# Gate and up weights loaded in runs of eight rows a partition: a decoder layer with a mixture of experts on one core

## What is computed

```python
t = x.reshape(bsz * s, d)                       # 512 x 1024, layer norm 1 done
g_logits = t @ router_group_w + router_group_b  # 4 groups: one is taken
e_logits = t @ router_expert_w + router_expert_b  # 32 experts: two of the group are taken
...
hg = jnp.einsum("td,edf->tef", t, exp_w_gate)   # gate and up weights: 32 x 1024 x 256 each
hu = jnp.einsum("td,edf->tef", t, exp_w_up)
hid = jax.nn.silu(hg) * hu * combine[:, :, None]
out = jnp.einsum("tef,efd->td", hid, exp_w_down)  # down weights: 32 x 256 x 1024
...
h = layer_norm(DEEPNORM_ALPHA * h + ffn, ln2_g, ln2_b)
```

## Time and profile before

| | |
|---|---|
| runs | 436.12, 437.76, 437.44 us |
| median | 437.44 us |
| profiled execution | 435.74 us, span of the trace 433.9 us |
| PE matmul busy | 409.5 us (94%) |
| PE weight loads busy | 276.5 us (64%) |
| VectorE, ScalarE, GpSimd busy | 187.3, 114.6, 83.5 us |
| mean granted PE clock | 0.983 of full speed |
| HBM read, written | 134.41 MB, 12.58 MB |

### The profile page before, as it was taken

How to read it: one execution, slowest core, us unless ns; L and a number is a source line. 1 busy time by engine, 2 the same in 40 slices (tenths; PEclk the granted TensorE clock), 3 DMA queues, 4 the chain that set the end, 5 groups by cost and what they waited for, 6 DMA issues and landing times.

```text
span 433.9 us, 6632 instructions
## 1 busy us (share of the span) xinstructions
PE 409.5 (94%) x2578; PEld 276.5 (64%) x2578; DVE 187.3 (43%) x368; ACT 114.6 (26%) x185; POOL 83.5 (19%) x113
## 2 busy tenths in 40 slices
PE   7999999999999999999999999999999878888793
PEld 6888877888888888865555555556555544453331
DVE  3569522699955388854222122212221212111077
ACT  4442387953132003211111111111111101001411
POOL 2220000000000001122332333233323311210124
PEclk9999999999999999999999999999999989898997
DMA  8865532033379999999999999999999999999584
GB/s 276 268 192 181 190 98 77 22 97 98 97 251 415 415 412 421 415 375 408 406 406 409 410 405 408 409 408 406 411 412 410 409 413 411 412 412 417 217 332 193
DMA packets 45569, 139.11 MB, mean 321 GB/s; under 512 B 5107, under 2 KB 17427, under 8 KB 41446
## 3 DMA queue, kind: packets, MB, share of 16 engines
q1 hardware_dynamic: 39376, 126.89, 75.3%
q0 software_dynamic: 6144, 11.84, 7.5%
q10 hardware_dynamic: 22, 0.02, 0.0%
HBM read 134.41 MB, written 12.58 MB: 339 GB/s over the span
## 4 chain that ended last, share of the span: by engine, by line
PE 80%; DMA 11%; DVE 5%; SPq 2%; issue 1%; ACT 0%; DVEq 0%; ACTq 0%
PE bank L1088 21%; PE bank L902 12%; PE bank L903 12%; PE bank L904 12%; PE bank L1117 10%; DMA wgu<-in_exp_w_up 5%; DMA wgu_first<-in_exp_w_up 5%; PE bank L1078 3%; PE bank L1108 2%; SPq L500 2%; PE bank L1179 2%; DVE stats L1572 1%; PE bank L885 1%; PE bank L1055 1%; PE bank L962 1%; DMA raw<-in_w_in 1%
## 5 line engine op out<-in xcount | busy, mean ns | idle before, releaser
L1088 PE MATMUL bank<-wgu,xTg 128*64 128x256 f32 x736 | 87.9, 394 | 7.5 <-DMA wgu<-in_exp_w_up 6.7
L1088 PEld LDWEIGHTS bank<-wgu,xTg 128*64 128x64 f32 x736 | 52.9, 141 | 35.2 <-DMA wgu<-in_exp_w_up 7.6
L902 PE MATMUL bank<-xT_hi,w_hi 128*128 128x512 f32 x160 | 63.0, 394 | 0.9 <-DVE xT_lo L1228 0.9
L903 PE MATMUL bank<-xT_lo,w_hi 128*128 128x512 f32 x160 | 62.4, 390 | 0.0
L904 PE MATMUL bank<-xT_hi,w_lo 128*128 128x512 f32 x160 | 62.4, 390 | 0.0
L1528 DVE TENSOR_TENSOR hid<-gated,bank 64x256 f32<-64x256 f32 x32 | 13.5, 423 | 112.1 <-ACT gated L834 112.0
L674 POOL DMA_INDIRECT y_pairs<-ys,y_rows x32 | 32.5, 1016 | 140.7 <-PE bank L1078 105.1
L834 ACT ACTIVATE gated<-bank 64x256 f32<-64x256 f32 x32 | 12.1, 377 | 136.8 <-PE bank L1088 136.8
L1117 PE MATMUL bank<-wdn,hidT 128*64 128x512 f32 x192 | 45.4, 593 | 0.0
L1205 DVE TENSOR_TENSOR w_lo<-raw,w_hi 128x2048 fp32r<-128x2048 f32 x12 | 27.5, 2288 | 26.6 <-ACT w_hi L748 26.6
L669 POOL DMA_INDIRECT xg<-h_rows,x_rows x31 | 31.4, 1014 | 24.7 <-issue 8.3
(11 more groups left out here) (255 smaller groups left out, 499.0 us busy)
## 6 DMA issues: line engine op xcount, KB each, us to landing
wgu<-in_exp_w_gate SPq DMA_DIRECT2D x24, 1024.0 KB, 19.9
wgu<-in_exp_w_up SPq DMA_DIRECT2D x24, 1024.0 KB, 21.8
wdn<-in_exp_w_down SPq DMA_DIRECT2D x24, 1024.0 KB, 21.5
raw<-in_w_in SPq DMA_DIRECT2D x9, 1024.0 KB, 5.3
raw<-in_w_out SPq DMA_DIRECT2D x4, 1024.0 KB, 5.0
wdn_extra<-in_exp_w_down SPq DMA_DIRECT2D x4, 1024.0 KB, 22.2
wgu_spare<-in_exp_w_gate SPq DMA_DIRECT2D x4, 1024.0 KB, 18.9
wgu_spare<-in_exp_w_up SPq DMA_DIRECT2D x4, 1024.0 KB, 21.2
```

The source lines that it names most:

```text
L902: pe.matmul(dst, a_hi, b_hi, start=start, stop=False)
L903: pe.matmul(dst, a_hi, b_lo, start=False, stop=False)
L1088: mm = pe.matmul(psum[2 + b][BLOCK * which:BLOCK * which + BLOCK, 0:F], xTg[b][:, j, h * BLOCK:(h + 1) * BLOCK], wgu[s][:, which, k, :], s ...
```

## The change

Gate and up weights are read as `(p k) f`: partition `p` gets rows 8p to 8p+7, one run of 8 KB. What multiplies them has to have the same order, so that step `k` of partition `p` is column 8p + k of the layer norm's result. The change gets it by writing that result in another order of columns: the left half of a row holds, for each `m` of 128, columns 8m to 8m+3, the right half columns 8m+4 to 8m+7. `h1_rows`, the gathers, `turn_x`, `take_first` and the products of the experts are as before and get the new order by that. It touches:

- `gu_of`, `gu_place`: the loads' form.
- the layer norm: L1363 writes to a new tile `scaled` (4 KB a partition more), and L1368 reads `scaled` and `ln_b` in the dealt order and writes `xres` contiguously.
- `turn_h1`: a transpose takes every fourth column, as in `turn_x`; the router's weights are loaded `(p k) n`.
- L1179: `h1` is read through `in_order`, which takes four floats from one half and four from the other by turns.

```diff
--- before.py
+++ after.py
@@ -165,6 +165,7 @@
         hidT = [sb(f"hidT{b}", [P, 2, BLOCK]) for b in range(2)]
         ys = [sb(f"ys{b}", [P, H]) for b in range(ROWS)]
         xg = [sb(f"xg{b}", [P, H]) for b in (1, 0)][::-1]
+        scaled = sb("scaled", [P, D])
         gelu_g = at("gelu_g", [P, CT, T], F32, shared)
         h1T = [at(f"h1T{b}", [P, KT, P], F32, shared + 4096 * b) for b in range(2)]
         shared_y = shared + 8192
@@ -407,6 +408,14 @@
         def static(i):
             return isinstance(i, int)
 
+        def dealt(rows, a):
+
+            return rows[:, :].rearrange("p (m a j) -> p a m j", a=2, j=4)[:, a, :, :]
+
+        def in_order(rows):
+
+            return rows.rearrange("p (a m j) -> p m a j", a=2, j=4)
+
         def halves_of(rows, n):
 
             return rows.rearrange("p (m j) -> p m j", j=4)[:, :, 2 * n:2 * n + 2]
@@ -414,14 +423,14 @@
 
         def gu_of(w, e):
             w = w[e:e + 1] if static(e) else w[bass.ds(e, 1)]
-            return w.rearrange("a (h p j) f -> p (a h) (j f)", h=2, p=P)
+            return w.rearrange("a (p k) f -> p (a k f)", p=P)
 
         def dn_of(e):
             w = exp_w_down[e:e + 1] if static(e) else exp_w_down[bass.ds(e, 1)]
             return w.rearrange("a (p j) d -> p (a j d)", p=P)
 
         def gu_place(s, which):
-            return wgu[s][:, which, :, :].rearrange("p (h j) f -> p h (j f)", h=2)
+            return wgu[s][:, which, :, :].rearrange("p k f -> p (k f)")
 
 
 
@@ -637,9 +646,9 @@
             pool.dma_start(ln_b[:, :], row(ln1_b).to_broadcast([P, D])).then_inc(ln1_in, 16)
             pool.wait_ge(gates_in, 32)
             pool.wait_ge(ln1_in, 32)
-            pool.dma_start(wr[:, :, 0:N_GROUPS], router_group_w.rearrange("(k p) n -> p k n", p=P)).then_inc(router_in, 16)
+            pool.dma_start(wr[:, :, 0:N_GROUPS], router_group_w.rearrange("(p k) n -> p k n", p=P)).then_inc(router_in, 16)
             pool.wait_ge(router_in, 16)
-            pool.dma_start(wr[:, :, N_GROUPS:NR], router_expert_w.rearrange("(k p) n -> p k n", p=P)).then_inc(router_in, 16)
+            pool.dma_start(wr[:, :, N_GROUPS:NR], router_expert_w.rearrange("(p k) n -> p k n", p=P)).then_inc(router_in, 16)
             pool.dma_start(rbias[:, 0:N_GROUPS], row(router_group_b).to_broadcast([P, N_GROUPS])).then_inc(router_in, 16)
             pool.dma_start(rbias[:, N_GROUPS:NR], row(router_expert_b).to_broadcast([P, N_EXP])).then_inc(router_in, 16)
 
@@ -995,7 +1004,8 @@
                 for n in halves:
                     pe.wait_ge(h1_ready, 2 * t + n + 1)
                     for k in range(4):
-                        mm = pe.transpose(psum[4 + 2 * (t % 2) + n][:, k * P:(k + 1) * P], xres[:, t, (4 * n + k) * P:(4 * n + k + 1) * P], ident[:, :])
+                        cols = xres[:, t, n * H:(n + 1) * H].rearrange("p (m j) -> p j m", j=4)[:, k, :]
+                        mm = pe.transpose(psum[4 + 2 * (t % 2) + n][:, k * P:(k + 1) * P], cols, ident[:, :])
                     mm.then_inc(h1_turned, 1)
 
             def router(t):
@@ -1176,7 +1186,7 @@
             pe.wait_ge(diag_ready, 1)
             for t in range(TT):
                 for h in range(2):
-                    pe.matmul(psum[2 * t + h][:, :], diag[:, 0, :], h1[:, t, h * H:(h + 1) * H], start=True, stop=False)
+                    pe.matmul(psum[2 * t + h][:, :], diag[:, 0, :], in_order(h1[:, t, :])[:, h * H // 8:(h + 1) * H // 8], start=True, stop=False)
             pe.wait_ge(diag_ready, 1 + TOP_K * TT)
             for t in range(TT):
                 last = 0 if t < DVE_ADDED else TOP_K - 1
@@ -1360,12 +1370,12 @@
                 residual(TT + t)
                 take_moments(t, var_ready)
 
-                link(v.scalar_tensor_tensor(out=xres[:, t, :], in0=xres[:, t, :], scalar=moments[:, t, 0:1], in1=ln_g[:, :], op0=ALU.subtract, op1=ALU.mult))
+                link(v.scalar_tensor_tensor(out=scaled[:, :], in0=xres[:, t, :], scalar=moments[:, t, 0:1], in1=ln_g[:, :], op0=ALU.subtract, op1=ALU.mult))
                 v.wait_ge(dev_ready, t + 1)
                 link(v.reciprocal(rstd[:, t:t + 1], rstd[:, t:t + 1]))
                 for h in range(2):
                     part = xres[:, t, h * H:(h + 1) * H]
-                    v.scalar_tensor_tensor(out=part, in0=part, scalar=rstd[:, t:t + 1], in1=ln_b[:, h * H:(h + 1) * H],
+                    v.scalar_tensor_tensor(out=part.rearrange("p (m j) -> p m j", j=4), in0=dealt(scaled, h), scalar=rstd[:, t:t + 1], in1=dealt(ln_b, h),
                                            op0=ALU.mult, op1=ALU.add).then_inc(h1_ready, 1)
                 if t == 0:
                     v.wait_ge(router_in, 16 * 4)
```

## The result

Median before 436.39 us (436.11 to 437.76, 5 runs on the same chip), after **433.42 us** (432.27 to 434.14, 5 runs). The ratio is 0.9936 (95% interval 0.9911 to 0.9962), by it 2.8 us less (1.7 to 3.9). The forecast was 434.2 us, 3.2 less than the median of three runs it started from (437.44); that median of before is now 436.39 over five. The profiled execution took 432.90 us for a span of 431.1 (before 435.74 and 433.9).

What follows compares the result with a forecast made beforehand. The prediction took the weight transfer stream to set the end, since PE waits for the last seven experts' up weights. Packets -3.6, transposes +0.2 and residual products +0.2 gave -3.2 us: 437.44 to 434.2 us, range 431.2 to 437.0.

Steps and rivals of the forecast that it cites:

- What bounds: Last seven experts: PE waits for up weights, so the transfer stream sets the end; up to 10.5 us to gain.
- 9 ns a pair, 0.072 us a load: Gate and up loads: one 8 KB packet for two of 4 KB saves this; 3.6 us over 50 loads.
- The full 13 ns: Gate and up loads: upper bound per packet pair, without subtracting overlap; 0.104 us a load.
- the 0.038 us a load from the mixed stretch: Gate and up loads: lower bound, from 412 against 410 GB/s in the stretch of 330 to 395.
- the rival that the packets bring next to nothing: Gate and up loads: only the lower bound's 1.9 us less 0.4 is gained, giving 435.9 us; chance 0.22.
- 50 loads and not 64: Weight stream: the hole at 186 swallows the first 14 loads' 1.0 us; only experts 7 to 31 count, 3.6 us.
- Transposes +0.2: Router transposes: reading with a step of four floats makes weight loads 210 ns instead of 140, costing 0.2 us.
- L1189 +0.2: Residual products at the end: the moving operand's jumps between row halves cost 0.2 us.
- the slower rival: Residual products: PE fed at half rate, 7.11 us become 14.2, giving 441.1 us; chance 0.07.
- The clock: Last expert's product: a shorter wait brings full clock and 1.7 us more gain, giving 432.5 us; chance 0.28.
- all that stands behind 394.75 moves along: Tail: last down products, the load of h1 and the last scatter shift by the whole gain of the stream.
- Gathers: Gathers sharing engines with the queue: they come 1.2 us later, within 3.3 us of slack, so cost 0.

Runs made afterwards that it cites:

- e1: The kernel before with only the gate and up loads in runs of 8 KB, layer norm, router and end products unchanged: 433.36 us, ratio 0.9926.
- e4: The kernel before with 8 KB runs only in the 50 gate and up loads of experts 7 to 31: 433.06 us, ratio 0.9925.
- e9: The kernel before with gate and up weights in four runs of 2 KB a partition instead of two of 4 KB: 444.24 us, ratio 1.0192.
- e10: The kernel before with down weights in two runs of 4 KB a partition instead of one of 8 KB: 438.59 us, ratio 1.0062.
- e5: The kernel after, unchanged, measured once more as base for three other runs: 433.13 us, ratio 0.9924 against the kernel before.
- e3: The kernel before with 8 KB runs only in the 14 gate and up loads of experts 0 to 6: 436.08 us, ratio 0.9995.
- e2: The kernel after with its gate and up loads turned back to two runs of 4 KB: 436.82 us, ratio 1.0010 against the kernel before.
- e6: The kernel after with expert 7's gate load released earlier by its own semaphore, up load as before: 435.66 us, ratio 0.9963 against the kernel before.

## Why the prediction was right, point by point

- **What bounds.** "What comes out of the stream earlier comes off the end": e1, e4, e9 and e10 move the stream and the time follows, up and down.
- **9 ns a pair, 0.072 us a load.** B - A fell by 3.2 us (after), 3.3 (e1), 3.4 (e4) and 3.5 (e5) over 50 loads: 0.064 to 0.070 us a load, 8 to 9 ns a pair; the 0.7 us by which e3's B - A is off would be 0.014 us a load. The way to it, two packet durations less their overlap, held. A count without durations says the same: over the seven stretches from 133 to 161 the kernel after moved 1439 packets of 8 KB and e10 2800 of 4 KB, so one took 311 or 160 ns of an engine, and 2 x 160 - 311 = 9 ns. The full 13 ns and the 0.038 us a load from the mixed stretch both missed. By the Trainium skill's page "DMA: Bandwidth & Descriptors" the 50 loads would have brought an estimate of 1.5 us; the measured 3.2 to 3.5 us decide, and the rival that the packets bring next to nothing is out: e1's interval begins at 2.3 us.
- **50 loads and not 64.** Borne out by e3 and e4, within the reach of their runs. e9 suggests the other side, that the rule holds for savings only, but its late gather can stand for part of that.
- **Transposes +0.2.** L1008's weight loads take 210 ns (forecast 210), and column A grew by 0.3 us. The layer norm's second step takes 749 ns a half, 1.41 us for two as in the earlier trace rows: term 0 was right.
- **L1189 +0.2, and the slower rival.** The residual products take 7.10 us against 7.11: the term was 0, not 0.2, and the rival of 7 us more is out. The Trainium skill's page "SBUF — State Buffer" (the paragraph on cachelines), by which runs of four floats fill their lines, gave the 0 that was measured.
- **The clock.** Said as a rival of 0.28: the last product would come to full clock and give 1.7 us. In the trace of after it did, and here the argument was right in sign and wrong in two points. The reason, a wait between 1.67 and 2.10 us, doesn't decide: PE's timeline of the kernel after has

```profile
368.91 3.67 PE L1098 MATMUL bank<-wgu,xTg 128*64 128x256 f32 x32 [2.39 <-DMA wgu<-in_exp_w_up]
...
377.26 5.36 PE L1098 MATMUL bank<-wgu,xTg 128*64 128x256 f32 x32 [2.05 <-DMA wgu<-in_exp_w_up]
...
392.97 3.67 PE L1098 MATMUL bank<-wgu_first,xTg 128*64 128x256 f32 x32 [1.95 <-DMA wgu_first<-in_exp_w_up]
```

  full clock (2.4 GHz) after 2.39 us, half (1.2 GHz) after 2.05, full after 1.95; and e1 had its last product at 5.36 us after 2.02. And the 1.7 us don't all come off the end. Where the last product took 5.36 us the rest took 33.6 to 33.8 us; in the four of the table with 3.67 us and gate and up in runs of 4 or 8 KB and down in 8, it took 34.5 to 34.7. Some 0.7 to 1.1 us are given back, to the load of residual rows (2.4 us waited for at L1189), a longer last scatter and the pairs. The step "all that stands behind 394.75 moves along" failed by that much.
- **The sum.** Forecast -3.6 + 0.2 + 0.2 = -3.2 us. By the table it is -3.2 (stream) + 0.3 (order) - 1.7 (clock) + 0.7 (tail) = -3.9, while the runs say -2.8 (after) and -3.3 (e5). So the forecast hit partly by luck, since the clock's 1.0 us, which it left out, doesn't show fully in the runs. One execution has a profile in each case; whether the others of the same kernel had their last product at half clock, as e1's did, stays open. They did differ in PE's clock: its mean lies between 0.983 and 0.994 over the five of the kernel after, and the profiled one is the 0.994.
- **Gathers.** The term 0, from a slack of 3.3 us, was read in mid-phase. The gather that follows the loads of experts 7 and 8 is another one. It was issued at 193.20, PE needed it at 200.26 and got it at 201.48, 8.3 us after its issue; e1 (7.4) and e4 (8.5) waited too, before and e5 did not. But larger packets need not be the cause: e2 and e10, with gate and up in 4 KB, waited for it by 0.51 and 0.95 us as well, 7.6 and 8.0 us after its issue. No cost of it can be seen, since PE was still ahead of the stream; e6 shows what it costs when it is two experts earlier.

## What to carry to other kernels

Where a stream of loads sets the end, take the price of a packet from two stretches of the trace with different packet sizes, net of their overlap, and for a saving count only the loads behind the last place where the issuing queue itself waits. Before closing a gap in a stream, look which small transfer runs in that gap, and who waits for it. A faster step just ahead of a tail is worth less than its length, since other transfers are near the same date.

## What the runs showed of the hardware that I had not expected

- The fixed cost of a packet was about the same over a factor of four in size: 8 to 10 ns a packet and engine for the stream from 8 to 4 KB and from 4 to 2 KB, a rate of 415, 409 and 395 GB/s.
- A moving operand whose runs of four floats alternate between two places 2 KB apart cost nothing: 592 ns for 512 columns in L1189, and 7.10 us for the 16 against 7.11 contiguous.
- Idle time of the same length before a product came with either clock, 3.67 or 5.36 us for the same 32 matmuls, also between executions of nearly the same kernel (e1 and e4, after waits of 2.02 and 2.03 us).
- With larger packets SP got further ahead: it issued the residual rows' load 20.4 us before the last product's start (372.56 and 392.97), before the change 13.6 us (381.11 and 394.75), with the down weights in 4 KB too 11.2 us (386.25 and 397.49, e10), and with 2 KB packets 8.4 us (397.69 and 406.09). So how far ahead SP gets goes with the number of packets, and with it how early a load at the queue's end can start.
